# Five opening stages take the first layer's shift from VectorE row sums, TensorE forms their scale alone, and each attention unit's scores and values share one bank

## The chip, the cores and the metric

The kernel runs on one NeuronCore of a Trainium2 chip. The metric is device time in microseconds of one execution, lower is better; the median of several runs counts.

## The reference, cut to what matters

Two trunk layers are applied to 128 context tokens and 256 latent tokens, 2048 wide, all in float32.

```python
def trunk_layer(l, x, cond, ...):
    mod = jax.nn.silu(cond) @ w_ada[l] + b_ada[l]
    shift, scale, gate = jnp.split(mod[:, None, :], 3, axis=-1)
    h = rmsnorm(x, norm_pre[l]) * (1 + scale) + shift
    proj = h @ w_in[l]            # 5120 columns
    if l % 2 == 0:
        ...                       # q, k, v; 12 heads of attention; 2-D DFT of u_b
        o = concat([silu(g_a) * o_a, silu(g_b) * fourier_mix(u_b)])
    else:
        ...                       # pooling and spatial gating
    return x + gate * rmsnorm(o @ w_out[l], norm_post[l]), k, v
```

Context tokens are conditioned by `c_ctx`, latent tokens by `c`, so every shift and scale exists twice. For a block of 128 columns k, the shift is two sums over 2048 products for each of 128 columns.

## The kernel before

**The main product.** The three tiles of 128 tokens are held on chip. A float32 product is made of three passes over rounded parts: a high part of the activations by a high part of the weights (line 874), high by low (L875), low by high (L876), each a 128x128 by 128x512 matmul. One k-step is a block of 128 of the 2048 rows, for three token tiles: 9 matmuls. Weights come in halves of two k-steps: SyncE's queue loads `raw`, ScalarE rounds it to `w_hi` (L1090), VectorE subtracts to get `w_lo` (L1343). Three `w_hi`/`w_lo` buffers rotate.

**The opening.** Before the first layer's product can use block k, its scale and shift must exist, so the opening interleaves them with three output chunks (v and k kept or spilled to `partial`). It is cut into nine stages: 0 and 1 make one block each, stage b from 2 on makes blocks 2b-2 and 2b-1 and stretches over six k-steps, beginning at opening step a = 6(b-2). In one stage:

- TensorE makes scale and shift as column sums in two *visits* (`first_ada`, L908), after steps a and a+2. Each multiplies two 1 MB tiles of `w_ada` (`raw_first`, three buffers, and from the seventh tile on also `dot_raw`) into one bank, in four rows of 32.
- VectorE copies the bank out (L1445), TensorE turns it with `first_cols` after step a+3 (L921, four transposes), VectorE reduces and finishes (`col_sum`, `scale_t`, `shift_t`, L1459 to L1468).
- After steps a+4 and a+5 come the `h` of the two blocks: TensorE transposes (L953), ScalarE scales and shifts (L1149) and rounds (L1153), VectorE subtracts to `h_op` (L1546).
- After step a+1 VectorE adds three banks into `partial` (L1432, L1435).

The first block's `h_op` is read by step a+6, the first step of the next stage, the second by step a+7.

**What sets the order.** A table written by hand (`timetable`) gives each engine's program: after each opening step its entries come in the order in which they were put, and on odd steps the split of a weight half comes first. SyncE's loads are one list (`opening_loads`), issued in order; a tile's load waits until its buffer is free, and everything behind it waits with it. GpSimd's queue loads constants and the `ada_tiles` for the later gate and shift, also in order; it loads the DFT matrices (`dft_sb`, L788) when the last attention product is done.

**Attention** lies in chunks 3 to 7, 36 units of one head and one token tile. Unit u has `scores` (L989 to L993) after step 4+2u, VectorE's row maximum, ScalarE's exponential (L1195), `turn_p` (transposes of the probabilities, L999, copied by ScalarE, L1188) after 6+2u and `pv` (values, L1009, copied out by VectorE, L1585) after 7+2u. Each uses one of the two side banks 6 and 7 in turn. The row sums for later blocks (`weigh_row`, L1348) multiply a tile by the condition, laid out in every partition, and accumulate over a row.

## Time and profile before

| what | value |
|---|---|
| median of 3 runs | 1136.58 us |
| lowest, highest | 1135.16, 1136.97 us |
| the profiled execution, its own time | 1137.09 us |
| its span | 1135.3 us |
| mean granted TensorE clock | 0.991 |
| TensorE busy | 1102.2 us, 97% |
| VectorE busy | 697.2 us, 61% |
| ScalarE busy | 417.1 us, 37% |
| DMA, mean | 213 GB/s |

The span runs from the first to the last instruction; 1.8 us of the execution's own time lie around it. Matmul ends are modelled, so the distance between the starts of two matmuls tells more than their durations. The times in the rows are from the span's start.

### The profile page before, as it was taken

How to read it: one execution, taken by the hardware profiler on the slowest of the kernel's cores; microseconds unless marked ns; L12 is line 12 of the kernel's file. 1: busy time of each engine (PE TensorE's matmuls, PEld its weight loads, DVE VectorE, ACT ScalarE, POOL GpSimd, SP SyncE). 2: the span in 40 equal slices, each digit the busy share in tenths (PEclk: the TensorE clock that was granted, in tenths of full speed). 3: DMA queues.
4: the chain of work that ended last, by engine and by line, in shares of the span. 5: the costliest groups of instructions: out<-in, count | busy, mean ns of one | idle time of the engine just before them, and what ended most of it. 6: DMA issues, size and time to landing. Idle time of an engine off the chain costs nothing.

```text
span 1135.3 us, 13583 instructions
## 1 busy us (share of the span) xinstructions
PE 1102.2 (97%) x5360; PEld 879.5 (77%) x5360; DVE 697.2 (61%) x1031; ACT 417.1 (37%) x653; POOL 33.3 (3%) x65
## 2 busy tenths in 40 slices
PE   5999999999999998999999899999999999999997
PEld 3566677787887886788888788888888888888885
DVE  3444455777777785599964664566756765343335
ACT  4332333343455342233333872223343323243332
POOL 1000010000000000000020000000000000000000
PEclk8999999999999999999999999999999999999999
DMA  8988775554555457567876143546454645444423
GB/s 358 398 325 340 287 260 237 212 221 188 185 221 236 171 217 299 222 242 265 313 294 258 42 145 122 179 182 217 136 203 185 222 174 198 151 137 158 135 87 112
DMA packets 39328, 242.29 MB, mean 213 GB/s; under 512 B 4784, under 2 KB 4896, under 8 KB 13280
## 3 DMA queue, kind: packets, MB, share of 16 engines
q1 hardware_dynamic: 29232, 190.85, 44.6%
q0 software_dynamic: 7344, 46.29, 11.0%
q10 hardware_dynamic: 2688, 4.26, 1.4%
q8 instruction: 43, 0.70, 0.2%
q14 instruction: 21, 0.17, 0.0%
HBM read 237.67 MB, written 3.72 MB: 213 GB/s over the span
## 4 chain that ended last, share of the span: by engine, by line
PE 89%; DMA 5%; DVE 4%; ACT 1%; issue 1%; SPq 0%; DVEq 0%; POOL 0%; ACTq 0%
PE bank L874 25%; PE bank L876 25%; PE bank L875 24%; DMA raw_first<-in_ada_first 3%; PE bank L908 2%; PE bank L1009 2%; PE bank L929 1%; DMA dft_sb<-in_dft 1%; PE bank L1051 1%; PE bank L992 1%; PE bank L968 1%; DVE w_lo L1343 1%; PE bank L953 1%; PE bank L999 1%; DVE x L1383 1%
## 5 line engine op out<-in xcount | busy, mean ns | idle before, releaser
L874 PE MATMUL bank<-w_hi,h_op 128*128 128x512 f32 x1116 | 456.5, 409 | 3.4 <-DVE h_op L1546 2.9
L876 PE MATMUL bank<-w_hi,h_op 128*128 128x512 f32 x1116 | 438.0, 392 | 0.0
L875 PE MATMUL bank<-w_lo,h_op 128*128 128x512 f32 x1116 | 437.0, 392 | 0.0
L1343 DVE TENSOR_TENSOR w_lo<-raw,w_hi 128x1024 fp32r<-128x1024 f32 x224 | 274.1, 1224 | 197.8 <-ACT w_hi L1090 197.5
L1090 ACT ACTIVATE w_hi<-raw 128x1024 fp32r<-128x1024 f32 x224 | 235.1, 1055 | 262.0 <-PE bank L876 244.2
L874 PEld LDWEIGHTS bank<-w_hi,h_op 128*128 128x128 f32 x1116 | 211.1, 189 | 63.9 <-issue 22.1
L876 PEld LDWEIGHTS bank<-w_hi,h_op 128*128 128x128 f32 x1116 | 210.4, 188 | 46.1
L875 PEld LDWEIGHTS bank<-w_lo,h_op 128*128 128x128 f32 x1116 | 211.3, 189 | 39.0
L874 PE MATMUL bank<-w_hi,o_low 128*128 128x512 f32 x192 | 75.9, 395 | 0.0
L876 PE MATMUL bank<-w_hi,o_low 128*128 128x512 f32 x192 | 74.9, 390 | 0.0
L875 PE MATMUL bank<-w_lo,o_low 128*128 128x512 f32 x192 | 74.8, 389 | 0.0
L1348 DVE SCALAR_TENSOR_TENSOR dot_raw<-dot_raw,cond_sb 128x2048 f32<-128x2048 f32 x32 | 73.2, 2287 | 0.0
L1149 ACT ACTIVATE silu<-bank,shift_t,scale_t 128x128 f32<-128x128 f32 (+1 forms) x58 | 26.4, 505 | 69.1 <-PE bank L953 63.8
L1188 ACT ACTIVATE probs_t<-bank 128x384 f32<-128x384 f32 (+1 forms) x36 | 15.1, 419 | 75.6 <-PE bank L999 75.6
L876 PEld LDWEIGHTS bank<-w_hi,o_low 128*128 128x128 f32 x192 | 36.1, 188 | 7.6
L874 PEld LDWEIGHTS bank<-w_hi,o_low 128*128 128x128 f32 x192 | 36.1, 188 | 7.2 <-DVE w_lo L1343 0.2
L875 PEld LDWEIGHTS bank<-w_lo,o_low 128*128 128x128 f32 x192 | 36.1, 188 | 7.1
L1348 DVE SCALAR_TENSOR_TENSOR late_junk<-raw,cond_half 128x1024 bf16<-128x1024 f32 x32 | 39.0, 1220 | 1.3 <-DMA cond_half<-cond_rows 1.3
L1348 DVE SCALAR_TENSOR_TENSOR raw<-raw,cond_half 128x1024 f32<-128x1024 f32 x32 | 39.0, 1220 | 0.0
L1546 DVE TENSOR_TENSOR h_op<-silu,h_op 128x384 fp32r<-128x384 f32 x29 | 16.2, 559 | 35.8 <-ACT h_op L1153 35.5
L1348 DVE SCALAR_TENSOR_TENSOR shift_junk<-dot_raw,cond_sb 128x2048 bf16<-128x2048 f32 x16 | 36.7, 2295 | 0.0
L1348 DVE SCALAR_TENSOR_TENSOR mixed<-dot_raw,cond_sb 128x2048 bf16<-128x2048 f32 x16 | 36.5, 2278 | 0.0
(200 smaller groups left out, 850.9 us busy)
## 6 DMA issues: line engine op xcount, KB each, us to landing
raw<-in_w_in SPq DMA_DIRECT2D x68, 1024.0 KB, 5.0
dot_raw<-in_ada_tiles POOLq DMA_DIRECT2D x32, 1024.0 KB, 5.1
raw<-in_w_out SPq DMA_DIRECT2D x32, 1024.0 KB, 4.9
raw_first<-in_ada_first SPq DMA_DIRECT2D x25, 1024.0 KB, 9.4
raw<-in_ada_groups SPq DMA_DIRECT2D x16, 1024.0 KB, 6.6
raw<-in_ada_halves SPq DMA_DIRECT2D x16, 1024.0 KB, 4.8
raw<-in_w_in SPq DMA_DIRECT2D x24, 512.0 KB, 7.0
dot_raw<-in_ada_first SPq DMA_DIRECT2D x7, 1024.0 KB, 6.6
```

What stands on the lines that cost most here:

```text
L874: pe.matmul(out, operand(layer, kind, 0, k, t), hi, start=k == begin, stop=False)
L875: pe.matmul(out, operand(layer, kind, 0, k, t), lo, start=False, stop=False)
L876: last = pe.matmul(out, operand(layer, kind, 1, k, t), hi, start=False, stop=k == end)
L908: last = pe.matmul(out[32 * j:32 * j + 32, 0:n_], cond[:, ks * part + k_, :], slot[:, n_ * k_:n_ * (k_ + 1)], start=part == 0 and k_ < 4, ...
L929: last = pe.matmul(out[32 * j:32 * j + 32, :], cond[:, 4 * q + j, :], raw[:, n_ % RAW, CW * j:CW * (j + 1)], start=q % 2 == 0, stop=q % 2 ...
L1009: last = pe.matmul(out[:, 0:HD], probs_t[:, s * P:(s + 1) * P], v, start=s == 0, stop=s == len(values) - 1)
L1090: act.activation(w_hi[:, half % WRING, :, :].rearrange("p k n -> p (k n)"), src, ACT.Copy)\
L1149: last = act.activation(full[:, lo_:hi_], side_bank(e)[:, lo_:hi_], ACT.Identity, bias=shift_t[:, k, c_:c_ + 1], scale=scale_t[:, k, c_:c_ ...
L1188: freed(act.activation(probs_t[:, 0:n], side_bank(e)[:, 0:n], ACT.Copy), e)
L1343: dve.tensor_tensor(w_lo[:, half % WRING, :, :].rearrange("p k n -> p (k n)"), src, hi, ALU.subtract)\
L1348: return dve.scalar_tensor_tensor(out=product, in0=tile, scalar=1.0, in1=cond_row, op0=ALU.mult, op1=ALU.mult, accum_out=total)
L1546: dve.tensor_tensor(h_op[:, 1, k, :], h_full[k % 2], h_op[:, 0, k, :].bitcast(F32), ALU.subtract)\
```

## The change

1. In stages 3, 4, 6, 7 and 8 (`ROW_STAGES`) the shift is made by VectorE. Its weights come as two row tiles (`ada_rows`, one for each block), and each takes two row sums (`first_dot`), one for each condition: placed after steps a-2, a-1, a+1 and a+2. The condition is broadcast to all partitions once more, early (`cond_first`, 2 MB written). TensorE forms the scale alone, in one visit after step a+2, with 16 products of 256 columns instead of 8 and 8 of 512, and two transposes in place of four. The number of 1 MB tiles is unchanged: four a stage.
2. ScalarE takes the SiLU of the condition's flat form at the very start, and stores it then.
3. Attention: `attend` n holds the values of unit n-2 and the scores of unit n in one bank; `turn_p` n-1 follows it. ScalarE, not VectorE, copies the values out, behind the exponential.
4. The DFT matrices are loaded after 14 of the `ada_tiles`, not after 18.
5. TensorE gets 5 and 8 more warming products before its first k-step, and the first `ada_cols` come one step later.

```diff
+BEFORE_DFT = sum(c * KT + s < (FIRST + 4) * KT + KT - 2 for c, s in GATE_AT) // 2 + DOT_SLOTS
+VALUES_LAG = 2
...
-SLOTS = [2 * len(ks) for ks in STAGES]
-PAIR = [len(ks) for ks in STAGES]
+ROW_STAGES = (3, 4, 6, 7, 8)
+BLOCKS_OF = [len(ks) * (1 if b in ROW_STAGES else 2) for b, ks in enumerate(STAGES)]
+SLOTS = BLOCKS_OF
+VISITS = [1 if b in ROW_STAGES else 2 for b in range(len(STAGES))]
...
     pre(0, "norm_rest")
+    pre(0, "warm", OPENING[0][0], 5)
...
     pre(0, "first_weights", 1)
+    pre(0, "warm", OPENING[0][0], 8)
...
-        for i in range(2):
-            first(at_ + 2 * i, "first_ada", b, i)
+        if b in ROW_STAGES:
+            for n in range(4):
+                first(at_ + (-2, -1, 1, 2)[n], "first_dot", STAGES[b][n // 2], n % 2)
+            first(at_ + 2, "first_ada", b, 0)
+        else:
+            for i in range(2):
+                first(at_ + 2 * i, "first_ada", b, i)
...
-    for u in range(HEADS * TOKS):
-        put(FIRST, begin + 2 * u + 2, "turn_p", u)
-        put(FIRST, begin + 2 * u + 3, "pv", u)
...
-    for u in range(HEADS * TOKS):
-        put(FIRST, begin + 2 * u, "scores", u)
+    for n in range(HEADS * TOKS + VALUES_LAG):
+        put(FIRST, begin + 2 * n, "attend", n)
+        if 0 < n <= HEADS * TOKS:
+            put(FIRST, begin + 2 * n, "turn_p", n - 1)
+        if n < HEADS * TOKS:
+            put(FIRST, begin + 2 * n, "exp", n)
...
                         old = list(nth_first)[n - FIRST_RAW - (n > EXTRA_AT)]
-                        if old in not_last:
+                        if old[0] == "first_row":
+                            sp.wait_ge(first_dotted, 2 * (FIRST_ROWS.index(old[1]) + 1))
+                        elif old in not_last:
                             sp.wait_ge(first_used, not_last.index(old) + 1)
...
-            pool.dma_start(cond_fl[:, :], cond_flat).then_inc(cond_fl_in, 16)
             wait_h(pool, 0, 0)
+            pool.wait_ge(cond_saved, 16)
+            pool.dma_start(cond_first[:, :, :], cond_rows.partition_broadcast(P)).then_inc(cond_first_in, 16)
...
-            load_tiles(DOT_SLOTS, KT + DOT_SLOTS)
-
-            wait_full(pool, "pv", len(units) - 1)
+            load_tiles(DOT_SLOTS, BEFORE_DFT)
+
+            wait_full(pool, "attend", len(units) + VALUES_LAG - 1)
             pool.dma_start(dft_sb[:, :], dft).then_inc(dft_in, 16)
-            load_tiles(KT + DOT_SLOTS, 2 * KT)
+            load_tiles(BEFORE_DFT, 2 * KT)
...
+                    if b in ROW_STAGES:
+
+                        dve.wait_ge(first_dotted, 2 * (FIRST_ROWS.index(STAGES[b][-1]) + 1))
+                        shift = shift_t[:, ks, :]
...
+                elif what == "first_dot":
+                    k, c_ = e[1:]
...
+                    if not c_:
+                        dve.wait_ge(first_raw_in[first_slot(nth)], 16 * first_turn(nth))
+                    tile = first_place[first_slot(nth)]
+                    weigh_row(tile if c_ else first_junk[:, :].bitcast(BF16), tile, cond_first[:, c_, :],
+                              shift_t[:, k, c_:c_ + 1]).then_inc(first_dotted, 1)
...
-                elif what == "pv":
-                    g, t, i = units[e[1]]
-                    h = 4 * g + i
-                    wait_full(dve, *e)
-                    freed(dve.tensor_copy(mixed[:, t, h * HD:(h + 1) * HD], side_bank(e)[:, 0:HD]), e)
```

VectorE, stage 4 of the opening, from the `h_op` of stage 3's first block (line numbers are those of each version's own file). Before:

```order
L1546 TENSOR_TENSOR h_op<-silu,h_op 128x384
L1343 TENSOR_TENSOR w_lo<-raw,w_hi 128x1024
L1546 TENSOR_TENSOR h_op<-silu,h_op 128x384
L1343 TENSOR_TENSOR w_lo<-raw,w_hi 128x1024
L1435 TENSOR_TENSOR partial<-bank,partial 128x512 x3
L1445 COPY rows<-bank 128x512
L1343 TENSOR_TENSOR w_lo<-raw,w_hi 128x1024
L1459 TENSOR_REDUCE col_sum<-bank 128x8
```

And of the change:

```order
L1605 TENSOR_TENSOR h_op<-silu,h_op 128x384
L1388 SCALAR_TENSOR_TENSOR first_junk,shift_t<-raw_first,cond_first 128x2048
L1383 TENSOR_TENSOR w_lo<-raw,w_hi 128x1024
L1605 TENSOR_TENSOR h_op<-silu,h_op 128x384
L1388 SCALAR_TENSOR_TENSOR raw_first,shift_t<-raw_first,cond_first 128x2048
L1383 TENSOR_TENSOR w_lo<-raw,w_hi 128x1024
L1388 SCALAR_TENSOR_TENSOR first_junk,shift_t<-raw_first,cond_first 128x2048
L1475 TENSOR_TENSOR partial<-bank,partial 128x512 x3
L1388 SCALAR_TENSOR_TENSOR raw_first,shift_t<-raw_first,cond_first 128x2048
L1485 COPY rows<-bank 128x256
L1383 TENSOR_TENSOR w_lo<-raw,w_hi 128x1024
L1500 TENSOR_REDUCE col_sum<-bank 128x4
```

Four row sums now stand between the first `h_op` and the copy of the bank, the first of them ahead of the second block's `h_op`.

GpSimd's queue where the DFT matrices are loaded, in the middle of the `ada_tiles`. Before:

```order
L742 DMA dot_raw<-in_ada_tiles 128x2048
L742 DMA dot_raw_76<-in_ada_tiles 128x2048
L742 DMA dot_raw<-in_ada_tiles 128x2048
L742 DMA dot_raw_76<-in_ada_tiles 128x2048
L788 DMA dft_sb<-in_dft 128x1156
```

And of the change:

```order
L812 DMA dft_sb<-in_dft 128x1156
L764 DMA dot_raw<-in_ada_tiles 128x2048
L764 DMA dot_raw_76<-in_ada_tiles 128x2048
L764 DMA dot_raw<-in_ada_tiles 128x2048
L764 DMA dot_raw_76<-in_ada_tiles 128x2048
```

The load stands four tiles earlier in the queue.

## Rows read from the trace of the kernel before

**Rows 1.** The page, part 1: busy time, share of the span, instructions.
```profile
PE 1102.2 (97%) x5360; PEld 879.5 (77%) x5360; DVE 697.2 (61%) x1031; ACT 417.1 (37%) x653; POOL 33.3 (3%) x65
```

**Rows 2.** The page, part 4: the chain that ended last, by line.
```profile
PE bank L874 25%; PE bank L876 25%; PE bank L875 24%; DMA raw_first<-in_ada_first 3%; PE bank L908 2%; PE bank L1009 2%; PE bank L929 1%; DMA dft_sb<-in_dft 1%; PE bank L1051 1%; PE bank L992 1%; PE bank L968 1%; DVE w_lo L1343 1%; PE bank L953 1%; PE bank L999 1%; DVE x L1383 1%
```

**Rows 3.** Windows of the opening: length, busy by engine, granted clock, DMA share, GB/s.
```profile
14.00:16.00 2.00, 0.75 (x16) 0.21 (x8) 2.00 (x6) 2.00 (x4) 0.00 (x0) 0.92 0.99 408
16.00:18.00 2.00, 1.92 (x16) 0.59 (x16) 1.11 (x3) 1.08 (x2) 0.00 (x0) 0.50 1.05 420
...
26.00:28.00 2.00, 2.00 (x35) 1.01 (x33) 0.00 (x0) 0.00 (x0) 0.00 (x0) 1.00 0.34 131
28.00:30.00 2.00, 2.00 (x15) 1.42 (x8) 0.42 (x1) 0.00 (x0) 0.00 (x0) 1.00 0.69 160
...
35.00:40.00 5.00, 4.76 (x31) 2.67 (x29) 3.46 (x5) 2.57 (x3) 0.00 (x0) 1.00 1.00 417
```

**Rows 4.** TensorE's timeline: start, us, line, tiles, shape, count, idle before.
```profile
39.50 1.06 PE L908 MATMUL bank<-raw_first,cond 128*32 128x512 f32 x8 [0.24 <-DMA raw_first<-in_ada_first]
...
83.52 0.47 PE L874 MATMUL bank<-w_hi,h_op 128*128 128x512 f32 x1 [0.20 <-DVE h_op L1546]
85.45 0.40 PE L876 MATMUL bank<-w_hi,h_op 128*128 128x512 f32 x1
87.63 0.50 PE L874 MATMUL bank<-w_hi,h_op 128*128 128x512 f32 x1
...
96.01 0.60 PE L921 MATMUL bank<-ident,gate 128*128 128x128 f32 x4
96.36 0.48 PE L874 MATMUL bank<-w_hi,h_op 128*128 128x512 f32 x1
```

**Rows 5.** VectorE's timeline, `h_op` of the first block: stages 2, 4, 5 and 8.
```profile
45.69 0.56 DVE L1546 TENSOR_TENSOR h_op<-silu,h_op 128x384 fp32r<-128x384 f32 x1 [1.73 <-ACT h_op L1153]
...
82.82 0.56 DVE L1546 TENSOR_TENSOR h_op<-silu,h_op 128x384 fp32r<-128x384 f32 x1 [3.61 <-ACT h_op L1153]
...
100.61 0.56 DVE L1546 TENSOR_TENSOR h_op<-silu,h_op 128x384 fp32r<-128x384 f32 x1 [3.30 <-ACT h_op L1153]
...
154.79 0.56 DVE L1546 TENSOR_TENSOR h_op<-silu,h_op 128x384 fp32r<-128x384 f32 x1 [3.30 <-ACT h_op L1153]
```

**Rows 6.** VectorE's timeline: pieces of known length, row sums among them.
```profile
28.44 0.42 DVE L1445 COPY gate<-bank 128x256 f32<-128x256 f32 x1 [4.25 <-PE bank L908]
...
36.26 1.89 DVE L1432 COPY partial<-bank 128x512 f32<-128x512 f32 x3 [0.82 <-PE bank L876]
...
429.28 2.28 DVE L1348 SCALAR_TENSOR_TENSOR dot_raw<-dot_raw,cond_sb 128x2048 f32<-128x2048 f32 x1
431.49 1.22 DVE L1343 TENSOR_TENSOR w_lo<-raw,w_hi 128x1024 fp32r<-128x1024 f32 x1
432.63 2.29 DVE L1348 SCALAR_TENSOR_TENSOR mixed<-dot_raw,cond_sb 128x2048 bf16<-128x2048 f32 x1
```

**Rows 7.** DMA issues: the condition's later broadcast, from issue to landing.
```profile
cond_sb<-cond_rows POOLq DMA_DIRECT2D x1, 2048.0 KB, 7.9
```

**Rows 8.** TensorE's timeline and a window around the DFT matrices' load.
```profile
447.75 0.39 PE L876 MATMUL bank<-w_hi,h_op 128*128 128x512 f32 x1
452.38 1.00 PE L1015 MATMUL bank<-dft_sb,v_nat 128*128 128x256 f32 x2 [4.24 <-DMA dft_sb<-in_dft]
456.09 0.39 PE L875 MATMUL bank<-w_lo,h_op 128*128 128x512 f32 x1
...
453.00:456.00 3.00, 3.00 (x8) 2.33 (x8) 1.22 (x2) 1.33 (x2) 0.00 (x0) 0.50 0.00 0
```

**Rows 9.** Attention, 165 to 440 us: groups by line and shape.
```profile
L1009 PE MATMUL bank<-v_nat,probs_t 128*128 128x128 f32 x120 | 19.4, 275 | 0.8 <-ACT probs L1195 0.8
...
L1585 DVE COPY mixed<-bank 128x128 f32<-128x128 f32 x36 | 10.4, 288 | 10.5 <-PE bank L1009 10.5
...
L1188 ACT ACTIVATE probs_t<-bank 128x128 f32<-128x128 f32 x12 | 3.3, 278 | 27.3 <-PE bank L999 27.3
```

More of the change, by code:

```diff
@@ L187, in timetable @@
     first(3, "first_ada", 2, 1)
-    first(3, "cond_silu")
-    first(5, "cond_save")
     first(4, "first_cols", 2)
@@ L362, in hybrid_step, with parts @@
         used[b] += 1
+    def parts(b):
+        if b in ROW_STAGES:
+            return [("first_row", k) for k in STAGES[b]] + [("first_ada", b, i) for i in range(SLOTS[b])]
+        return [("first_ada", b, i) for i in range(SLOTS[b])]
     def opening_loads():
@@ L393, in hybrid_step @@
         [("first_ada", e[1], PAIR[e[1]] * e[2] + i) for e in side if e[0] == "first_ada" for i in range(PAIR[e[1]])]
-    nth_first = {x: n for n, x in enumerate(x for x in loads if x[0] == "first_ada")}
-    not_last = [x for x in nth_first if x[2] < SLOTS[x[1]] - 1]
-    ring = [x for x in loads if x[0] != "first_ada"]
+    nth_first = {x: n for n, x in enumerate(x for x in loads if x[0] in ("first_ada", "first_row"))}
+    not_last = [x for x in nth_first if x[0] == "first_ada" and x[2] < SLOTS[x[1]] - 1]
+    assert [x[1] for x in nth_first if x[0] == "first_row"] == FIRST_ROWS
+    ring = [x for x in loads if x not in nth_first]
     nth_load = {x: n for n, x in enumerate(ring)}
@@ L675, in _ @@
             for what in loads:
-                if what[0] == "first_ada":
+                if what in nth_first:
                     n = nth_first[what]
@@ L913, in side_product @@
                             last.then_inc(first_used, 1)
-                    if not i:
+                    if i < VISITS[b] - 1:
                         return
@@ L917, in side_product @@
                     b = e[1]
-                    wait_free(pe, "first_ada", b, 1)
+                    wait_free(pe, "first_ada", b, VISITS[b] - 1)
                     pe.wait_ge(const_in, 16)
-                    for i in range(SLOTS[b]):
+                    for i in range(BLOCKS_OF[b]):
                         last = pe.transpose(out[:, i * P:(i + 1) * P], (rows, gate)[b % 2][:, i * P:(i + 1) * P],
@@ L1563, in part @@
                                             ALU.subtract), e)
-                elif what == "scores":
+                elif what == "attend":
+                    if e[1] >= len(units):
+                        return
                     u = e[1]
```

168 lines of the change are left out of this document (99 added, 69 removed).

## The prediction

> **What bounds the kernel now.** I read the page first. TensorE is busy for 97% of the span, VectorE for 61% [rows 1], and the chain that ended last runs for three quarters through the matmuls of lines 874 to 876; two entries in it are transfers: the opening's tiles with 3% and the DFT matrices with 1% [rows 2]. So a change pays if it takes work from TensorE or ends one of its waits, and costs if it makes TensorE wait. Then I read the stages that are touched. In the opening, the windows show DMA full at 417 GB/s from 35 to 40 us, and only 0.34 and 0.69 busy from 26 to 30 us [rows 3]. At 39.50 us TensorE waits 0.24 us for a tile that has just landed [rows 4]: there TensorE and DMA are in balance, with nothing to spare. Later stages keep a steady beat, seen best in VectorE's `h_op` of each stage's first block: 82.82, then 100.61 us, a period of 17.79 us [rows 5].
>
> **Part 1, what TensorE saves.** A visit of 8 products costs 87.63 - 85.45 = 2.18 us between two matmul starts, less the 0.24 us that one matmul takes anyway (83.52 to 85.45 us hold eight starts): 1.94 us. Four transposes cost 96.36 - 96.01 = 0.35 us, so two fewer save 0.18 us [rows 4]. The remaining visit has twice the products of half the width, so it costs what one visit cost. Taken alone, five stages save 5 x 2.12 = 10.6 us of TensorE.
>
> **Part 1, what VectorE adds.** Four row sums a stage. One holds the engine for 431.49 - 429.28 = 2.21 us, a `w_lo` split for 432.63 - 431.49 = 1.14 us, three additions into `partial` take 1.89 us (1.81 until the next starts), the copy of 256 columns 0.42 us where 512 took more [rows 6]; `h_op` takes 0.56 us and its follower can start after 0.48 [rows 5]. The order of the instructions decides, so I walk one stage from the start of the first block's `h_op` (0):
>
> - `h_op` to 0.48, row sum to 2.69, split to 3.83, second `h_op` ends at 4.39. TensorE began step a at 83.52 - 82.82 = 0.70, and is through it at 87.63 - 1.94 - 82.82 = 2.87 [rows 4, 5]. Step a+1 reads the second `h_op`: it waits until 4.53 (0.14 us after the end, as at 83.52). The first pause is 1.66 us, which is nearly the visit that was removed there.
> - Row sum from 4.31 to 6.52, split to 7.66, row sum to 9.87, `partial` to 11.68, row sum to 13.89, copy ends at 14.31.
> - TensorE: steps a+1 and a+2 to 8.7, the visit to 10.65, step a+3 to 12.7. The transposes wait for the copy until 14.37: a second pause of 1.6 us.
> - From the transposes to the next first `h_op` it is 100.61 - 96.01 = 4.60 us [rows 4, 5], less 0.18: the next begins at 18.79.
>
> The period of such a stage is thus 18.8 us, not 17.8: the loop runs through VectorE, although VectorE is busy for only some 16 of these 18.8 us. Stage 5 keeps both visits and its 17.8 us. From stage 2's `h_op` (45.69) to stage 8's (154.79) were 109.1 us, two waits for tiles among them [rows 5]; now 5 x 18.8 + 17.8 = 111.8 us. **+2.7 us.** DMA has more time per stage than before, since each period grows and the number of tiles stays, so those two waits go into the pauses; a row tile's buffer comes free when VectorE has done both sums, and the next use is a stage later.
>
> **Part 1, the early broadcast.** It writes 2.1 MB between the tiles that TensorE is about to need. At 417 GB/s [rows 3] that is 5.0 us of all DMA engines; the later broadcast took 7.9 us from issue to landing [rows 7]. It is issued behind the first `h_op`, at about 23 us, and fills the hole from 26 to 30 us, which is 2 x 0.66 + 2 x 0.31 = 1.9 us deep [rows 3]. The rest, 3.1 us, moves every later landing, and the tile that TensorE waited for at 39.50 us has no slack. Bounds: 0, if the order of queues lets the tiles pass it, and 5.0. I take **+3.2 us**, and as TensorE then idles some 3 us in the twenties to forties, an even chance of a fall of its clock, whose price is 1.8 us (below): **+0.9 us**.
>
> **Parts 2 and 5.** The earlier SiLU takes a table load out of ScalarE's queue, where ScalarE was waiting for TensorE anyway: nothing. The warming products fill two pauses near 15 and 21 us; the granted clock is 0.92 of full from 14 to 16 us and 0.50, the lower level, from 16 to 18 [rows 3]. If they keep the 2.4 GHz, the first k-step comes 2 to 3 us earlier; if not, they delay it by up to 2 us. Either way TensorE then meets the transfers at 39.50 us, so both are hidden as long as DMA is full. I take 0; the gain would show only if the broadcast cost nothing.
>
> **Part 4, the DFT matrices.** From 447.75 to 456.09 us TensorE made one matmul start, the DFT product and seven more starts: 8.34 us, where at 0.24 us each and as much for the product (an estimate from its 256 columns) it is 2.2 us. Most of it is the wait for `dft_sb`, 4.4 us beyond the time of the matmul at 447.75, the rest, 1.8 us, is that the clock then ran at half, 0.50 from 453 to 456 us [rows 8]. Four tiles earlier in its queue, the load is issued when attention ends, after step 14 of chunk 7; its use stands after step 3 of chunk 9, 21 k-steps of at least 2.1 us later, some 44 us. The whole is saved, as VectorE has idle time on both sides: **-6.2 us** (bounds -4.2 and -6.5).
>
> **Part 3, attention.** The same products are made, so TensorE saves only waits: 0.8 us on ScalarE's copies of the probabilities are in the rows, as a value product followed them after one step and now follows after two. VectorE loses 36 copies, 10.4 us, ScalarE gains 36 of some 278 ns [rows 9], behind the exponential, ahead of the release of the bank; both engines have room at 61% and 37% [rows 1]. Bounds 0 and -2.5 us; I take **-1.0 us**.
>
> **Sum.** +2.7 + 3.2 + 0.9 - 6.2 - 1.0 = -0.4 us. The profiled execution took 1137.09 us, which gives 1136.7; the median of the runs is 0.5 us lower, and against it the forecast is 1136.2 us. A measurement of this kernel can tell about 0.2%, 2.3 us, from no change, so this is "within".
>
> **The rivals.**
>
> 1. *The row sums are hidden.* For it speaks VectorE's 61% [rows 1]; against it the order: a row sum stands ahead of an `h_op` that TensorE needs next. Then the opening gets its 10.6 us instead of losing 2.7: 1136.2 - 13.3 = 1122.9 us. Chance 0.08.
> 2. *The broadcast finds room.* If transfers ahead of 39.50 us have slack that the wait of 0.24 us hides, or the tiles go first, 3.2 + 0.9 us fall away: 1132.1 us, and with 2 us kept from the warm start 1130.1. Chance 0.17.
> 3. *TensorE's clock falls in the new pauses* (the slower side). Each row stage has two, of 1.66 and 1.6 us. The place is the second, ahead of the transposes: step a+4 behind it lies on the loop, the work behind the first has 1.6 us of slack. A fall there costs 1.8 us as in [rows 8], for one to five stages +1.8 to +9.0 us; with three, 1141.6 us. It decides from the second fall on. The rows show falls after 4.24 us of waiting [rows 8], and before 16 us after shorter gaps among small products [rows 3]; the 0.24 us at 39.50 did nothing. The Trainium skill, "TensorE: Matmul & The Clock Gate", section "Why this matters for your kernels", puts the fall down to idle gaps longer than these pauses; by that, none would come in the row stages and this rival would be empty. The fall at 16 us, after gaps of about one microsecond, does not agree with it, so I keep a chance of 0.15.
>
> **How the numbers follow.** The forecast has 0.60, with its own range of 1133.0 to 1139.4 us from the bounds of the broadcast, the clock and attention; a sixth of it lies below 1134.3, a ninth above 1138.9. Faster by over 0.2%: 0.08 + 0.17 + 0.10 = 0.35. Slower: 0.15 + 0.07 = 0.22. Within: 0.43. The range 1129.5 to 1142.0 leaves out rival 1 and the far half of rival 3.
>
> **What would show it.** Right: periods of 18.8 us between the first `h_op` of stages 3, 4, 6, 7 and 8 and of 17.8 for stage 5; TensorE waiting for VectorE's second `h_op` and again for the copy; `h_op` of stage 2 near 49.7 us; no wait and full clock at the DFT product. Wrong: periods near 16 us (rival 1); stage 2's `h_op` at or before 45.7 us (rival 2); a granted clock below 1.00 between 50 and 160 us (rival 3); a wait for the DFT matrices, or a new wait of TensorE for ScalarE in attention.

## The result, and the profile after

The change takes 1141.47 us (median of 4 runs, 1140.71 to 1143.0) against 1136.78 us (1135.16 to 1137.44) of the kernel before, run beside it (with one run more than the three above): a ratio of 1.0046, 95% interval 1.003 to 1.0062. It is slower by about 5 us. The forecast was 1136.2 us, "within", with the measured time inside its range. So the sum was wrong by some 5 us, towards the slower side that rival 3 stood for, but not by that rival's mechanism.

The profiled execution took 1140.71 us, its span is 1138.9 us, 3.6 us more than before. The page, part 1 (busy time by engine) and part 4 (the chain), to be held against [rows 1, 2]:

```profile
PE 1092.2 (96%) x5376; PEld 880.2 (77%) x5376; DVE 729.5 (64%) x1035; ACT 421.8 (37%) x688; POOL 33.3 (3%) x65
...
PE bank L898 25%; PE bank L900 24%; PE bank L899 24%; DMA raw_first<-in_ada_first 5%; PE bank L1013 1%; PE bank L932 1%; PE bank L953 1%; DVE w_lo L1383 1%; DVE first_junk L1388 1%; PE bank L1077 1%; PE bank L992 1%; PE bank L1029 1%; PE bank L1036 1%; PE bank L977 1%; DVE x L1423 1%
```

TensorE is busy for 10.0 us less and the span is 3.6 us longer: the work that was taken off came back as waits, and more. In the chain the opening's tiles have gone from 3% to 5%, and the row sums (`first_junk`) appear with 1%.

Where the time went is read from the same instruction in both traces, VectorE's `h_op` of each stage's first block (start, us, engine, line). Stages 2, 3, 4, 5, 6, 7 and 8:

```profile
50.18 0.56 DVE L1605 TENSOR_TENSOR h_op<-silu,h_op 128x384 fp32r<-128x384 f32 x1 [1.72 <-ACT h_op L1178]
...
68.96 0.56 DVE L1605 TENSOR_TENSOR h_op<-silu,h_op 128x384 fp32r<-128x384 f32 x1 [2.82 <-ACT h_op L1178]
...
87.98 0.56 DVE L1605 TENSOR_TENSOR h_op<-silu,h_op 128x384 fp32r<-128x384 f32 x1 [3.06 <-ACT h_op L1178]
...
105.77 0.56 DVE L1605 TENSOR_TENSOR h_op<-silu,h_op 128x384 fp32r<-128x384 f32 x1 [3.30 <-ACT h_op L1178]
...
124.56 0.56 DVE L1605 TENSOR_TENSOR h_op<-silu,h_op 128x384 fp32r<-128x384 f32 x1 [2.83 <-ACT h_op L1178]
...
144.54 0.56 DVE L1605 TENSOR_TENSOR h_op<-silu,h_op 128x384 fp32r<-128x384 f32 x1 [3.32 <-ACT h_op L1178]
...
163.43 0.56 DVE L1605 TENSOR_TENSOR h_op<-silu,h_op 128x384 fp32r<-128x384 f32 x1 [2.92 <-ACT h_op L1178]
```

Against [rows 5], stage 2 comes 50.18 - 45.69 = 4.49 us later. From there to stage 8 it is 113.25 us where it was 109.10: another 4.15 us. The opening thus loses 8.64 us. The periods are 18.78, 19.02, 17.79 (stage 5), 18.79, 19.98 and 18.89 us. The same comparison on ScalarE's roundings of the weights (L1116, before L1090) still gives about +8.6 us when attention begins. Here are two of them, one when attention is nearly over and one behind the DFT product, each in the kernel before and then in the change:

```profile
425.71 1.06 ACT L1090 ACTIVATE w_hi<-raw 128x1024 fp32r<-128x1024 f32 x1 [1.79 <-PE bank L876]
435.60 1.06 ACT L1116 ACTIVATE w_hi<-raw 128x1024 fp32r<-128x1024 f32 x1 [1.79 <-PE bank L900]
...
458.16 1.06 ACT L1090 ACTIVATE w_hi<-raw 128x1024 fp32r<-128x1024 f32 x1
461.96 1.06 ACT L1116 ACTIVATE w_hi<-raw 128x1024 fp32r<-128x1024 f32 x1
```

The lag is +9.89 us, then +3.80 us, and about that to the end. So attention lost 1.25 us and the DFT matrices gave 6.1 us back.

Each of these figures comes from one execution, and the opening differs between executions. x5 below has the program of the kernel before up to the end of attention, and in its trace stage 2 starts at 45.09 and stage 8 at 152.80 us (45.69 and 154.79 before). x4 has the opening of the change, and its stages 2 and 8 start at 50.77 and 163.07 us (50.18 and 163.43). Differences of 1 to 2 us between single traces are no more than that.

TensorE's timeline shows the waits of the opening (in brackets the idle time ahead and who ended it):

```profile
32.25 1.30 PE L932 MATMUL bank<-raw_first,cond 128*32 128x512 f32 x8 [3.57 <-DMA raw_first<-in_ada_first]
36.11 1.93 PE L932 MATMUL bank<-raw_first,cond 128*32 128x512 f32 x8 [2.57 <-DMA raw_first<-in_ada_first]
...
110.20 0.50 PE L898 MATMUL bank<-w_hi,h_op 128*128 128x512 f32 x1 [1.40 <-DVE h_op L1605]
120.14 0.41 PE L945 MATMUL bank<-ident,rows 128*128 128x128 f32 x2 [1.01 <-issue]
128.99 0.50 PE L898 MATMUL bank<-w_hi,h_op 128*128 128x512 f32 x1 [1.42 <-DVE h_op L1605]
136.99 1.07 PE L932 MATMUL bank<-raw_first,cond 128*32 128x256 f32 x16 [2.60 <-DMA raw_first<-in_ada_first]
```

The two waits at the top are for tiles behind the broadcast. The next three are the pauses that the prediction described, for the second `h_op` (1.40 and 1.42 us) and for the copy of the bank (1.01 us, put down to "issue"). The last is one that it had not priced: a row stage waiting for its own tile. SyncE issued that tile here:

```profile
128.49 0.33 SPq L737 DMA_DIRECT2D raw<-in_w_in  x1
128.86 0.43 SPq L713 DMA_DIRECT2D raw_first<-in_ada_first  x1
```

Ahead of it in the list stands a half of the weights, whose buffer comes free when VectorE has split the half that lies in it (`w_lo`, 127.24 to 128.46 us), and a row sum now stands ahead of that split. In each of the five row stages this tile is issued 4.31 us behind the stage's first `h_op`, and it lands 5.7 to 8.1 us later. TensorE waits for it 0.25, 1.65, 0.19, 2.60 and 1.51 us.

Windows of the opening (length, busy by engine, granted clock, DMA share, GB/s), to be held against [rows 3]:

```profile
26.00:28.00 2.00, 1.86 (x10) 1.28 (x8) 0.10 (x1) 0.00 (x0) 0.00 (x0) 1.00 1.07 455
28.00:30.00 2.00, 0.55 (x3) 0.31 (x3) 0.47 (x4) 1.20 (x3) 0.00 (x0) 1.00 1.01 426
30.00:32.00 2.00, 0.00 (x0) 0.00 (x0) 1.34 (x2) 1.19 (x2) 0.00 (x0) 1.00 0.96 406
32.00:34.00 2.00, 1.30 (x8) 0.19 (x8) 0.44 (x1) 0.00 (x0) 0.00 (x0) 0.74 1.00 397
34.00:36.00 2.00, 0.00 (x0) 0.00 (x0) 0.00 (x0) 0.00 (x0) 0.00 (x0) 0.50 1.02 412
36.00:38.00 2.00, 1.89 (x9) 0.22 (x9) 0.00 (x0) 0.00 (x0) 0.00 (x0) 0.50 1.00 416
```

The hole of DMA from 26 to 30 us is gone: the broadcast has nothing to fall into. TensorE, whose clock is full up to 32.9 us, stands for two stretches and then works at 0.50 up to 39.8 us.

### The profile page after: what moved, and what is told of

The parts are those of the page before. It is cut to its first block, busy times and chain, and to the rows that moved or that the text cites. A ratio compares the mean times of both kernels' runs of the same rounds, so it can differ in the third digit from the quotient of the medians.

```text
span 1138.9 us, 13643 instructions
## 1 busy us (share of the span) xinstructions
PE 1092.2 (96%) x5376; PEld 880.2 (77%) x5376; DVE 729.5 (64%) x1035; ACT 421.8 (37%) x688; POOL 33.3 (3%) x65
## 4 chain that ended last, share of the span: by engine, by line
PE 87%; DMA 5%; DVE 5%; ACT 2%; issue 1%; SPq 0%; DVEq 0%; ACTq 0%
PE bank L898 25%; PE bank L900 24%; PE bank L899 24%; DMA raw_first<-in_ada_first 5%; PE bank L1013 1%; PE bank L932 1%; PE bank L953 1%; DVE w_lo L1383 1%; DVE first_junk L1388 1%; PE bank L1077 1%; PE bank L992 1%; PE bank L1029 1%; PE bank L1036 1%; PE bank L977 1%; DVE x L1423 1%
## 5 line engine op out<-in xcount | busy, mean ns | idle before, releaser
L1116 ACT ACTIVATE w_hi<-raw 128x1024 fp32r<-128x1024 f32 x224 | 235.3, 1056 | 268.0 <-PE bank L900 250.2
```

Of the source, the lines that this page charges most:

```text
L1116: act.activation(w_hi[:, half % WRING, :, :].rearrange("p k n -> p (k n)"), src, ACT.Copy)\
```

## The experiments

Each is made from the changed kernel unless its diff says otherwise; "stage 2" is the start of that stage's first `h_op`.

### The first layer's shift taken back: x1, x2, x3

x1 has no row stages and no early broadcast. Attention, the DFT matrices, the SiLU and the warming products stay.

```diff
-ROW_STAGES = (3, 4, 6, 7, 8)
+ROW_STAGES = ()
...
-            pool.dma_start(cond_first[:, :, :], cond_rows.partition_broadcast(P)).then_inc(cond_first_in, 16)
```

> The changed kernel without part 1: all nine stages keep both visits, and the early broadcast is gone; the attention, DFT, SiLU and warming parts stay. My theory says that part 1 costs about 10 us in this kernel (the broadcast about 4, the row stages about 4 to 5) and that the rest gains: DFT -6.1 us, attention +1.3 us, the warm start -1 to -2 us. Expected: 1130 to 1131.5 us, stage periods of 17.8 us, the first h_op of stage 2 at 44 to 45 us. The rival, that the loss sits in attention or elsewhere, expects 1137 us or more.

Measured: 1130.24 us (1128.9 to 1131.69), ratio 0.9939 [0.9924, 0.9954]. Stage 2 at 43.71 us, then periods of 17.8 us but for 18.1 and 18.4 in the first two. So the row sums with their broadcast cost 11 us, and all other parts together gain 6.5 us. x1 also shows that DMA has no hole from 26 to 30 us without the broadcast:

```profile
26.00:28.00 2.00, 1.95 (x10) 1.37 (x8) 0.02 (x1) 0.00 (x0) 0.00 (x0) 1.00 1.02 420
28.00:30.00 2.00, 1.61 (x11) 0.50 (x11) 0.55 (x4) 1.11 (x3) 0.00 (x0) 1.00 0.98 399
```

x2 keeps the broadcast of x1's removed part, and nothing reads it.

> As x1_no_rows, but the early broadcast of the condition is still loaded, and nobody reads it. The price of the broadcast alone: 2.1 MB at 417 GB/s are 5.0 us of DMA, of which up to 1.9 us fall into the hole at 26 to 30 us. Theory: 3 to 5 us more than x1_no_rows, with waits of TensorE for tiles between 28 and 40 us. Rival (the transfers have slack, the late h_op of stage 2 comes from something else): within 1 us of x1_no_rows.

Measured: 1137.5 us (1135.27 to 1138.53), ratio 1.0004 [0.9993, 1.0014], 7.3 us over x1: more than either reading had. Stage 2 of x1 and of x2, and TensorE's waits for tiles ahead of it:

```profile
31.28 1.06 PE L929 MATMUL bank<-raw_first,cond 128*32 128x512 f32 x8 [1.36 <-DMA raw_first<-in_ada_first]
...
43.71 0.56 DVE L1600 TENSOR_TENSOR h_op<-silu,h_op 128x384 fp32r<-128x384 f32 x1 [1.73 <-ACT h_op L1175]
```

```profile
33.21 1.94 PE L932 MATMUL bank<-raw_first,cond 128*32 128x512 f32 x8 [4.53 <-DMA raw_first<-in_ada_first]
36.47 1.94 PE L932 MATMUL bank<-raw_first,cond 128*32 128x512 f32 x8 [1.32 <-DMA raw_first<-in_ada_first]
...
51.71 0.56 DVE L1605 TENSOR_TENSOR h_op<-silu,h_op 128x384 fp32r<-128x384 f32 x1 [1.73 <-ACT h_op L1178]
```

In this pair of traces the broadcast alone moves stage 2 by 8.0 us. Over all traces the size is less sharp: in the seven with a warm start and no broadcast ahead of stage 2 (x1, x8, x12 to x16) that stage starts at 43.71 to 45.40 us, in the six with both (the change, x2, x3, x4, x6, x9) at 50.18 to 51.71 us. The two groups are 4.8 to 8.0 us apart, and the medians of x1 and x2 say 7.3 us.

x3 is the change with row sums over the first 1024 of 2048 products. Its shift of ten blocks lacks the other half of the products.

```diff
-                    weigh_row(tile if c_ else first_junk[:, :].bitcast(BF16), tile, cond_first[:, c_, :],
+                    weigh_row(tile[:, 0:HALF_K] if c_ else first_junk[:, 0:HALF_K // 2].bitcast(BF16), tile[:, 0:HALF_K], cond_first[:, c_, 0:HALF_K],
```

> The changed kernel with each row sum over the first 1024 of its 2048 weights only (the shift of ten blocks is therefore computed from half of the products). All transfers, visits and waits stay; each of the four sums is 1.1 us shorter. Theory (the loop through VectorE sets the period of a row stage): periods fall from 18.8 us to 16 to 17.3 us, the wait of TensorE for the second h_op disappears, and the whole takes 1130 to 1134 us, with waits for tiles as the next limit. Rival (the tiles' landing sets the period already): periods stay above 18 us and the time stays near 1141 us.

Measured: 1132.83 us (1131.6 to 1140.6), ratio 0.997 [0.9953, 0.9986]. The periods are 16.59, 18.02, 17.80, 16.66, 17.11 and 17.62 us, 103.8 us in all against the change's 113.25. Halving a row sum takes 9.4 us from the row stages, so VectorE's work is what makes them long. They do not all come down to the 16.6 us of the shortest: in three of the five TensorE waits 0.81 to 1.68 us for a tile.

### Where the broadcast's 8 us come from: x10, x11

x10 is x1 without the 13 warming products, x11 is x2 without them.

```diff
-    pre(0, "warm", OPENING[0][0], 5)
...
-    pre(0, "warm", OPENING[0][0], 8)
```

> x1_no_rows (no row sums, no early broadcast) without the 5 and 8 extra warming products ahead of the first k-step. In x1 stage 2's first h_op starts at 43.71 us, in the kernel before at 45.69 us, where TensorE's clock is at half from 16 to 25 us and DMA has a hole from 26 to 30 us. Theory (the warm start keeps the buffers turning, so that DMA never idles; that is worth the 2.0 us): h_op of stage 2 at 45.7 us, the hole is back, opening about 3.4 us longer, 1132.5 to 1134 us. Rival (the 2.0 us come from the earlier SiLU or its store, and the warming products do nothing): h_op at 43.7 us, 1130 us.

> x2_broadcast_only without the 13 extra warming products: the early broadcast meets a cold start, as the working of the prediction had it. With the warm start the broadcast moves stage 2's h_op by 8.0 us (43.71 to 51.71). Theory (5.0 us are its bytes, as DMA is full from 14 us on in x1; the rest is the clock's fall in the pauses of 4.5 and 1.3 us and what TensorE then has to catch up): with a cold start the hole of 1.9 us takes part of the bytes, so the broadcast moves h_op by 3 to 6 us against x10, to 49 to 51.5 us, and this kernel is no slower than x2, 1135 to 1137.5 us. Rival (the broadcast costs its 8 us whatever the start, by the order in the queues): h_op at 53 to 54 us, 1139 to 1140.5 us.

Measured: x10 1132.0 us (1130.98 to 1132.91), x11 1135.88 us (1133.58 to 1139.22). With x1 and x2 this makes a table of two by two:

| stage 2, us (median of the runs, us) | no broadcast | broadcast |
|---|---|---|
| without the warming products | 44.78 (1132.0) | 48.81 (1135.88) |
| with them | 43.71 (1130.24) | 51.71 (1137.5) |

In these traces the warming products are worth 1.1 us at stage 2 when there is no broadcast, and cost 2.9 us when there is one. Each is a difference of two executions. x10's 44.78 us lies within the 43.71 to 45.40 us of the warm traces, so the gain of 1.1 us is not clear of that spread; x11's 48.81 us lies 1.4 us or more ahead of every trace with the broadcast and a warm start. Windows of x10, where DMA's hole is back, and of x11, where the broadcast fills it:

```profile
26.00:28.00 2.00, 2.00 (x31) 1.15 (x24) 0.43 (x1) 0.00 (x0) 0.00 (x0) 1.00 0.60 193
28.00:30.00 2.00, 1.91 (x10) 1.31 (x8) 0.05 (x1) 0.00 (x0) 0.00 (x0) 1.00 0.95 344
```

```profile
26.00:28.00 2.00, 2.00 (x24) 0.95 (x27) 0.00 (x0) 0.00 (x0) 0.00 (x0) 0.53 1.07 451
28.00:30.00 2.00, 2.00 (x21) 1.28 (x14) 0.43 (x1) 0.00 (x0) 0.00 (x0) 1.00 0.95 401
```

With a cold start the broadcast costs 4.0 us, which is close to the prediction's 3.2 + 0.9. With the change's warm start there is no hole. Then the tile of the second visit is there at 36.47 us (x2) instead of 34.97 us (x11), and from then on the clock stays at half for some 10 us instead of some 3.5 us (the cold start has a stretch at half of its own ahead of this, up to about 25 us in x10 and 28 us in x11). Why this tile lands 1.5 us later although DMA is full in both was not settled.

### What sets the length of a row stage: x6, x9

x6 puts the first row sum behind the second `h_op`; x9 puts it ahead of the first `h_op`, and the second sum behind the second `h_op`.

```diff
-                first(at_ + (-2, -1, 1, 2)[n], "first_dot", STAGES[b][n // 2], n % 2)
+                first(at_ + (-1, -1, 1, 2)[n], "first_dot", STAGES[b][n // 2], n % 2)
```

```diff
-                first(at_ + (-2, -1, 1, 2)[n], "first_dot", STAGES[b][n // 2], n % 2)
+                first(at_ + (-2 if b == 3 else -3, -1, 1, 2)[n], "first_dot", STAGES[b][n // 2], n % 2)
```

> The changed kernel with the first row sum of a row stage behind the second block's h_op instead of ahead of it. Theory (the loop of a row stage runs through VectorE, from the first h_op to the copy of the bank, and the order inside this stretch does not change its length): TensorE's wait of 1.4 us for the second h_op goes, the wait for the copy or for the visit's tile grows by as much, periods stay 18.8 to 20.0 us, 1140.5 to 1142 us. Rival (the pause ahead of the second h_op is what costs): periods of 17.4 us, five times -1.4 us, 1134.5 us.

> The changed kernel with the first of four row sums ahead of the first block's h_op, where VectorE is idle for 2.8 to 3.3 us (stages 4, 6, 7 and 8; stage 3 keeps its place), and the second one behind the second h_op. Theory (the stretch of VectorE from first h_op to the copy sets the period): it is 2.2 us shorter; the waits for the second h_op go, the period of stages 4, 6, 7 and 8 becomes 16.6 to 18 us (the rest is TensorE's own work of 15.7 us and the waits for tiles), 1133 to 1138 us, about 1135.5. Rival (the tiles' landing sets the period, as the last tile of a row stage is issued only some 4 us after the first h_op): periods of 18.8 us stay, the waits for tiles grow, 1140 to 1142 us.

Measured: x6 1150.34 us (1146.38 to 1153.78), ratio 1.0106 [1.0079, 1.0133]. Both readings missed it. The wait for the second `h_op` is gone, the wait for the copy has grown to 2.84, 3.19, 3.57, 3.21 and 2.17 us in the five row stages, and during or behind each of them the clock falls to 0.50. The trace is of the slowest of the four runs. VectorE's timeline of x6, from first `h_op` to copy to the next first `h_op`, and its TensorE with a window:

```profile
110.35 0.56 DVE L1605 TENSOR_TENSOR h_op<-silu,h_op 128x384 fp32r<-128x384 f32 x1 [3.30 <-ACT h_op L1178]
...
125.02 0.42 DVE L1485 COPY rows<-bank 128x256 f32<-128x256 f32 x1
...
131.20 0.56 DVE L1605 TENSOR_TENSOR h_op<-silu,h_op 128x384 fp32r<-128x384 f32 x1 [4.09 <-ACT h_op L1178]
```

```profile
125.54 0.66 PE L945 MATMUL bank<-ident,rows 128*128 128x128 f32 x2 [3.57 <-issue]
...
126.00:128.00 2.00, 2.00 (x6) 1.61 (x6) 1.05 (x5) 0.00 (x0) 0.00 (x0) 0.50 0.81 287
```

In the change the stretch from `h_op` (105.77) to the copy (119.62) is 13.85 us; here it is 14.67 us, since VectorE now idles for ScalarE's second `h` instead of adding in that time. From the copy to the next `h_op` it is 6.18 us instead of 4.94, with the clock at 0.50. One row stage is 20.85 us long instead of 18.79. The two pauses of 1.4 and 1.0 us in the change were harmless to the clock; those of 2.17 to 3.57 us here were not.

x9: 1139.73 us (1138.09 to 1143.11), ratio 1.0024 [1.0012, 1.0035], 1.7 us faster than the change. The periods of stages 4, 6, 7 and 8 are 18.21, 17.38, 17.70 and 18.21 us against 19.02, 18.79, 19.98 and 18.89. The stretch of VectorE set the period, as the theory said; now the waits for tiles do (1.75 to 2.25 us in three of them). From stage 2 to stage 8 the trace is 5.2 us shorter than that of the change, the medians differ by only 1.7. In the trace, stage 2 starts 1.4 us later than in the change, with the same program ahead of it (the spread between executions), and at 327.94 us the wait of attention (below) is followed by a fall of the clock, which costs another 1.6 us.

### Attention: x4, x8

x4 puts the turn of the scale's columns (`ada_cols`) back to where it was before the change.

```diff
-        put(FIRST, 5 + 14 * (2 * g + 1) + 4, "ada_cols", g)
+        put(FIRST, 5 + 14 * (2 * g + 1) + 3, "ada_cols", g)
```

> The changed kernel with the turns of the second layer's scale (ada_cols) one step earlier again, where they stood before the change. In the changed kernel they follow, on an odd step, the attend whose bank they take, and TensorE waits 0.97 and 2.08 us for ScalarE's copy of the values. Theory: these two waits go, 1138 to 1139.5 us, 2 to 3 us less than the changed kernel. Rival: the wait only moves to the next user of the bank, and the time stays at 1141 us.

Measured: 1148.57 us (1148.28 to 1149.35), ratio 1.0101 [1.0086, 1.0116], 7.1 us slower than the change: a miss. TensorE's timeline of the change, then of x4:

```profile
246.01 0.65 PE L961 MATMUL bank<-ident,ada_row 128*128 128x128 f32 x4 [0.97 <-ACT mixed L1159]
331.71 0.66 PE L961 MATMUL bank<-ident,ada_row 128*128 128x128 f32 x4 [2.08 <-ACT mixed L1159]
```

```profile
245.70 1.12 PE L961 MATMUL bank<-ident,ada_row 128*128 128x128 f32 x4 [3.08 <-ACT mixed L1159]
335.03 1.12 PE L961 MATMUL bank<-ident,ada_row 128*128 128x128 f32 x4 [4.16 <-ACT mixed L1159]
```

Both waits are 2.1 us longer, one k-step, and both now end at half clock (1.12 us for the four transposes instead of 0.65). The step later is part of the change's cure, not a fault of it. The turn takes the bank of the last `attend`, which holds scores and values now, and ScalarE lets it go only after the exponential and the copy of the values (245.69 us, 0.27 us long; the turn starts at 246.01).

So the place to try is another step later. x8 does that on top of x1, and puts the turn ahead of that step's `attend`, so that it does not take that one's bank:

```diff
+    for g in range(GROUPS):
+        put(FIRST, 5 + 14 * (2 * g + 1) + 5, "ada_cols", g)
     for n in range(HEADS * TOKS + VALUES_LAG):
...
-        put(FIRST, 5 + 14 * (2 * g + 1) + 4, "ada_cols", g)
```

> x1_no_rows with the three ada_cols of attention one step later again, and ahead of that step's attend, not behind it. In x1 TensorE waits 1.01 and 2.09 us there for ScalarE to release the last attend's bank (exponential and copy of the values). Theory (the turn comes too early for this bank; a step of 2.1 us later the bank is free): both waits go, 1127.2 us. Rival (the turn now takes the bank that the next turn_p needs, so that TensorE waits for VectorE's reduction instead): within 0.5 us of x1, 1130.2 us.

Measured: 1127.59 us (1125.96 to 1128.39), ratio 0.9916 [0.9902, 0.9929]. That is 2.65 us less than x1, and the two turns wait for nothing (a new wait of 0.76 us for VectorE's `mods` stands behind the second):

```profile
235.05 0.60 PE L959 MATMUL bank<-ident,ada_row 128*128 128x128 f32 x4
318.61 0.66 PE L959 MATMUL bank<-ident,ada_row 128*128 128x128 f32 x4
```

### The DFT matrices alone: x5

The kernel before with the load four tiles earlier:

```diff
-            load_tiles(DOT_SLOTS, KT + DOT_SLOTS)
+            load_tiles(DOT_SLOTS, BEFORE_DFT)
...
-            load_tiles(KT + DOT_SLOTS, 2 * KT)
+            load_tiles(BEFORE_DFT, 2 * KT)
```

> The kernel before, with the DFT matrices' load four tiles earlier in GpSimd's queue and nothing else. The trace of the change shows no wait at the DFT product, and its lag behind the kernel before shrinks by 6.1 us there. Theory (the term of the prediction was right, and nothing takes it back later): 6.0 to 6.3 us faster, 1130.5 us. Rival (the four tiles that now come later make a mod or a row sum late, and part is given back): 1132 to 1135 us.

Measured: 1131.8 us (1129.21 to 1132.65), ratio 0.9952 [0.9938, 0.9965], 5.5 us faster than the 1137.28 us of the kernel before beside it. In its trace the lead grows by 6.1 us at the DFT product, from 2.0 to 8.1 us (the 2.0 us ahead of it are the spread of the opening). The term stands.

### Is the broadcast's price its bytes or its place: x12 to x16

x12 has row sums in stages 6, 7 and 8 alone and issues the broadcast behind stage 3's last `h`; x13 is x12 with the order of x9 and the turns of x8.

```diff
-ROW_STAGES = (3, 4, 6, 7, 8)
+ROW_STAGES = (6, 7, 8)
...
             wait_h(pool, 0, 0)
+            pool.dma_start(mod_c[:, :, :], mod_cols).then_inc(mod_in, 16)
+            wait_h(pool, 0, STAGES[3][-1])
             pool.wait_ge(cond_saved, 16)
             pool.dma_start(cond_first[:, :, :], cond_rows.partition_broadcast(P)).then_inc(cond_first_in, 16)
-            pool.dma_start(mod_c[:, :, :], mod_cols).then_inc(mod_in, 16)
```

> The changed kernel with row sums in stages 6, 7 and 8 alone, and the broadcast of the condition behind stage 3's last h instead of the first block's. From 50 to 160 us DMA is busy for 0.83 of the time in x1, which leaves 18.7 us of it, against the 5.0 us of the broadcast. Theory (the broadcast costs only where DMA is full; each row stage costs its longer loop through VectorE): stage 2's h_op at 43.7 us as in x1, then the periods of the change in stages 6 to 8 (18.79, 19.98 and 18.89 against 17.79 us), +4.3 us over x1, 1134.5 us. Rival (the broadcast delays tiles at any place): another 2 us or more between stages 3 and 6, 1136.5 us or more.

> x12 with the first row sum ahead of the first h_op and the second behind the second h_op (as in x9, where the periods of stages 6 to 8 were 17.38, 17.70 and 18.21 us) and with ada_cols of attention ahead of the attend (as in x8). Theory (with the broadcast at a free place and VectorE's stretch shortened, row stages and column stages take the same time, since tiles set both): within 1 us of x8, 1127.5 us. Rival (row stages pay for TensorE's saved 2.12 us each once nothing else waits): 1122 to 1125 us. Other rival (tiles of row stages come later than in x9, as TensorE is ahead): 1129 to 1131 us.

Measured: x12 1140.21 us (1133.03 to 1142.82), ratio 1.0016 [0.9997, 1.0036]; x13 1134.4 us (1126.68 to 1138.84), ratio 0.9964 [0.9938, 0.9991]. In the traces the theory of both failed on one wait (6.21 us in x12, 5.20 us in x13), here in x12 with windows ahead of it:

```profile
78.28 1.93 PE L933 MATMUL bank<-raw_first,cond 128*32 128x512 f32 x8 [6.21 <-DMA raw_first<-in_ada_first]
...
62.00:64.00 2.00, 2.00 (x11) 1.59 (x10) 1.61 (x2) 1.97 (x4) 0.00 (x0) 1.00 0.32 123
64.00:66.00 2.00, 2.00 (x16) 0.79 (x18) 1.38 (x3) 1.19 (x2) 0.53 (x1) 1.00 0.45 82
...
72.00:74.00 2.00, 0.07 (x4) 0.00 (x0) 0.00 (x0) 0.00 (x0) 0.00 (x0) 1.00 1.01 414
```

DMA idles from 62 to 66 us because SyncE's list stands still: its next entry, a half of the weights, waits 6.2 us for VectorE's split to free a buffer (until 64.04 us), and everything behind it waits with it. Then three tiles are issued within 2.4 us, and the broadcast, issued at 65.13 us, lands among them 13.3 us later. The mean share of 0.83 hid that. The row stages behind it took 18.80, 18.79 and 18.78 us, so 18.8 us is what a row stage costs when its tiles are in time. The single runs spread over about 10 us in x12 and 12 us in x13, and the trace of x12 is of the slowest of its ten. x12's fastest run took 1133.03 us and x13's 1126.68 us, so the collision seems not to cost this much in every execution; no trace shows a fast one.

x14 and x15 issue the broadcast in two halves of 1 MB, when TensorE has turned the first block's `h` of stages 4 and 5, ahead of the next two holes. x14 is otherwise x13; x15 is otherwise x8, and reads nothing of it.

```diff
-            wait_h(pool, 0, STAGES[3][-1])
-            pool.wait_ge(cond_saved, 16)
-            pool.dma_start(cond_first[:, :, :], cond_rows.partition_broadcast(P)).then_inc(cond_first_in, 16)
+            for i in range(2):
+                wait_full(pool, "h", 0, STAGES[4 + i][0])
+                pool.wait_ge(cond_saved, 16)
+                pool.dma_start(cond_first[:, i:i + 1, :], cond_rows[i:i + 1, :].partition_broadcast(P)).then_inc(cond_first_in, 16)
```

> x13 with the broadcast in two halves of 1 MB, issued when TensorE has turned the first block's h of stage 4 and of stage 5, ahead of the 2.4 us (at 81 us) and 2.5 us (at 99 us) in which DMA idles in each stage in x8. In x12 and x13 the one broadcast of 2 MB behind an h_op met three tiles that are issued in a burst there, and TensorE waited 6.2 and 5.2 us for one of them. Theory (a broadcast costs its bytes where tiles in flight are needed next, and nothing where it fills a hole of DMA): no wait above 1 us for tiles in stages 4 to 6, row stages of 17.4 us, 1127 us, within 1 us of x8. Rival (the tiles are late by the broadcast wherever it stands): waits for tiles in stages 5 and 6, 1130 us or more.

> x8 (no row sums) with the same two half broadcasts, which nothing reads. Theory: the price of 2 MB at free places is 0 to 0.5 us, 1127.6 us, against 7.3 us at the change's place (x2 against x1). Rival (bytes cost 2.5 us each wherever): 1130 to 1132.6 us.

Measured: x15 1127.57 us (1126.45 to 1128.22), ratio 0.9915 [0.9902, 0.9929]; x8 has 1127.59. **The same 2 MB that cost 7.3 us at the change's place cost nothing that the medians show in two holes.** In the traces x15 is 0.9 us behind x8, which the spread between executions covers. The place and the size of the pieces were changed together, so how much each of them gives is not shown. Windows of x8, then of x15:

```profile
80.00:82.00 2.00, 2.00 (x11) 1.60 (x10) 1.27 (x2) 2.00 (x4) 0.00 (x0) 1.00 0.54 225
82.00:84.00 2.00, 2.00 (x14) 1.05 (x17) 1.38 (x3) 1.63 (x3) 0.00 (x0) 1.00 0.32 43
```

```profile
80.00:82.00 2.00, 2.00 (x10) 1.61 (x9) 1.42 (x2) 1.97 (x5) 0.00 (x0) 1.00 0.95 356
82.00:84.00 2.00, 2.00 (x18) 0.42 (x16) 1.59 (x2) 0.72 (x1) 0.00 (x0) 1.00 0.83 248
```

x14: 1136.68 us (1135.02 to 1139.03), ratio 0.9995 [0.9985, 1.0006], a miss for a reason of its own: the second half landed at about 105 us, and the first row sum of stage 6, which this order puts ahead of stage 5's first `h_op`, waited 9.28 us for it. x16 issues both halves a stage earlier:

```diff
-                wait_full(pool, "h", 0, STAGES[4 + i][0])
+                wait_full(pool, "h", 0, STAGES[3 + i][0])
```

> x14 with the two half broadcasts a stage earlier, in stages 3 and 4. In x14 VectorE's first row sum of stage 6 waited 9.28 us for the second half, TensorE 8.07 us for the h_op behind it: the half was issued too late for its reader, which the expectation of x14 had overlooked. Theory: that wait goes, and with the clock's fall behind it some 10 us; the row stages take 17.4 us where tiles come in time and 18.2 us where they do not, 1126.5 to 1128.5 us, the same as x8 and x15. Rival (with the broadcast free, TensorE's saved 2.12 us of a row stage come through): 1122 to 1125 us. Other rival (waits of 1.7 to 2.0 us for the row stages' last tile, as in x14, cost TensorE's clock too): 1129 us or more.

Measured: 1129.0 us (1126.51 to 1131.49), ratio 0.9935 [0.9919, 0.995], 7.7 us ahead of x14. Its row stages take 17.37, 19.30 and 17.39 us. In the last two of the three TensorE waits 1.77 and 1.26 us for the visit's tile. The longer of these waits, with a window behind it:

```profile
126.03 1.07 PE L935 MATMUL bank<-raw_first,cond 128*32 128x256 f32 x16 [1.77 <-DMA raw_first<-in_ada_first]
...
128.00:130.00 2.00, 2.00 (x6) 1.51 (x6) 1.84 (x4) 0.00 (x0) 0.00 (x0) 0.50 0.59 109
```

The clock has fallen to half, as the other rival had it, and that stage is the long one; behind the wait of 1.26 us it stays full. Two of the row stages thus take 0.4 us less than column stages of 17.8 us, and one takes 1.5 us more. x8, which has no row stages, is still the fastest of all kernels here, beside x15.

## Why the prediction was wrong, and where it was right

The terms of the trace are +4.49 us up to stage 2, +4.15 us in the stages, +1.25 us in attention and -6.1 us at the DFT matrices: +3.8 us in sum, against +3.6 us in the span, where the prediction had -0.4. (The medians differ by 4.7 us.) Of the 4.2 us between, attention makes 2.25 us, the stages 1.45 us, the opening ahead of stage 2 0.4 us and the DFT matrices 0.1 us. So two steps failed: in attention the change was taken to remove waits only, and in the row stages the waits for tiles were taken to vanish in the pauses.

- **What TensorE saves** (10.6 us) was right in size: it is busy for 10.0 us less. None of it came through.
- **What VectorE adds**, the walk through a stage, was right in mechanism and size: 18.78 and 18.79 us in the two row stages of the change in which TensorE hardly waits for a tile, and 18.78 to 18.80 us in x12, against 18.8 forecast. The two pauses are there (1.40 to 1.44 us against 1.66, and 1.0 against 1.6). x3 and x9 confirm that VectorE's stretch sets the period.
- **The step that failed there** is "those two waits go into the pauses". The prediction looked at the buffers of the row tiles. What holds the visit's own tile back is the half of the weights ahead of it in SyncE's list, which waits for VectorE's split, and so for a row sum. TensorE waits for the tile 1.65, 2.60 and 1.51 us in three stages, which take 19.02, 19.98 and 18.89 us. The pauses do take the first 1.4 us of such a wait: with waits of 1.41 us (x4) and 1.38 us (x12) the stage still takes 18.78 us. The rest lengthens the stage, here by 0.23 + 1.19 + 0.10 = 1.5 us, which is the difference between +4.15 and +2.7 us. In x4, with the same opening, the six stages take 112.3 us instead of 113.25: how late a tile lands differs from execution to execution.
- **The early broadcast** was put at +3.2 and +0.9 us, and stage 2 at 49.7 us; it came at 50.18 us. This looks right, but by luck, as two errors cancel. The broadcast costs more than 4.1 us at stage 2 in this kernel: 50.18 - 43.71 = 6.5 us against x1, and 8.0 us in x2. The hole of 1.9 us that was to take part of it exists only after a cold start (x10; x1 has none), and the same change removes the cold start. The other error is the gain of the next point. (The working's own rest is 3.1 us, of which it makes 3.2, and it has the broadcast issued at about 23 us; the trace has it at 21.4.)
- **Parts 2 and 5** were put at nothing, "the gain would show only if the broadcast cost nothing". That was so, and it was counted on neither side: without the broadcast stage 2 comes 45.69 - 43.71 = 2.0 us earlier (1.8 to 2.0 us in five traces, 0.3 and 1.1 us in x13 and x14). That gain is lost to the broadcast.
- **The DFT matrices**: -6.2 us forecast, -6.1 us in the traces, -5.5 us in x5. Right.
- **Attention**, the largest miss: -1.0 us forecast, +1.25 us measured. The step that failed is "TensorE saves only waits": two new ones of 0.97 and 2.08 us came in, where `ada_cols` takes a bank that is now released behind the exponential and a copy on ScalarE. The prediction had read ScalarE's 37% as room. With these waits removed (x8) attention is 1.1 us better than in the kernel before: by the same roundings of the weights, x8 leads by 3.25 us when attention begins and by 4.36 us when it is nearly over. So the forecast gain is there once the turn stands where the bank is free.
- **Rival 1** did not happen. **Rival 2** was false at this place and true at another (x15). **Rival 3** did not happen in the change: the granted clock was 1.00 from 50 to 160 us. Its mechanism exists, though: in x6 the clock fell behind pauses of 2.17 us and more, in x16 behind one of 1.77 us.

## What to carry to other kernels

The mean share of a transfer engine says nothing about whether a transfer is free. Look for the stretches in which it idles, ask why it idles there (here: one load waits for its buffer, the list behind it waits too, and a burst of loads follows), and issue the extra transfer ahead of such a stretch, in pieces that fit it. When a tile lands late, look at what stands ahead of it in its queue before you look at its own buffer. When a change has several parts, ask whether one of them removes the room that another counts on. And when two results share a bank, its release moves to the later of the two readers: walk to the next user of that bank.
